# ScalarE's copies of the next weights among the squares, in the second down projection of a two-layer decoder trunk

## The chip, the cores and the metric

The kernel runs on one core of a Trainium2 chip. The metric is the device time of one execution in microseconds (us). TensorE's clock has two levels, 1.2 and 2.4 GHz; the profile gives the granted clock as a share of the higher one.

## What is computed

Two layers over 512 tokens of width 1024. Each layer has a token mixer (a gated linear recurrence in layer 0, attention with a forget bias in layer 1) and a squared-ReLU MLP with 4096 hidden features; each half is preceded by an RMS norm that is scaled and shifted by the conditioning vector. A last RMS norm ends it.

```
def sqrelu_mlp(h, w1, w2):
    a = jax.nn.relu(h @ w1)
    return (a * a) @ w2

for i in range(DEPTH):
    ...
    x = x + g1[:, None, :] * y
    h = modulate(x, norm2_w[i], sh2, sc2)
    x = x + g2[:, None, :] * sqrelu_mlp(h, mlp_w1[i], mlp_w2[i])
return rmsnorm(x, final_w)
```

The inputs are float32. The change concerns the last quarter of each MLP, the product with the second half of w2, and the sum of squares of the new x for the norm behind it.

## The kernel before

**Layout.** Activations lie transposed: features on the 128 partitions, the 512 tokens along the free dimension. x is 8 tiles of 128 features by 512 tokens. Every weight is cut into blocks of 128 x 1024 (512 KB), and four blocks are a quad; a layer has 26 quads, numbered through both layers. The blocks are streamed in one fixed order through four slots, j = 0 to 3, each with three buffers: `raw` (float32, from memory), `whi` (a copy in the matmul's reduced format, the high part) and `wlo` (raw less whi, the low part). Activations are split in the same way (h1hi and h1lo, a0hi and a0lo), and each product is three matmuls (lines 704 to 706): high by high, high weight by low activation, low weight by high activation. One block against one set of 8 activation tiles is 24 matmuls.

**The life of a slot.** SyncE loads raw[j] when the low part of the block before it in that slot has been made. ScalarE copies raw[j] to whi[j] when TensorE has ended the block that used the slot and the load has landed. GpSimd makes wlo[j] (line 622) behind that copy. TensorE waits for both before the block (`split`). The copy is the helper `hi_ahead`, lines 320 to 323:

```
def hi_ahead(quad, j):

    act.wait_ge(pe_blk, quad * 4 + j + 1)
    act.wait_ge(raw_in[j], quad * 16 + 32)
    S.activation(whi[:, j, :], raw[:, j, :], ACT.Copy).then_inc(w_hi, 1)
```

`pe_blk` counts TensorE's ended blocks. `hi_ahead(quad, j)` fills the slot that block j of this quad has just freed, for block j of the next quad. Each engine runs its own program in order; the order of ScalarE's operations is written out by hand.

**The MLP** (`mlp`, one function for each engine) has four stages, twice up and down: up projection of 16 hidden tiles (4 quads), down projection of these (4 quads), then the same for the other half of the hidden features. In a down projection a feature tile of the output needs two blocks, so a quad holds two features; feature t is summed in bank 4 + t % 2, and before it starts TensorE waits for VectorE's update of x with feature t - 2. In the first down projection of a layer ScalarE does nothing but `hi_ahead(q, j)` for each slot in turn, and VectorE updates x at line 1402.

**The second down projection** is part of `turnover(n, ...)`, with n = 2 in layer 0 and n = 4 in layer 1 (`from_w_out(n)` is false). It has four quads, q0 to q0 + 3. Features 0 to 5 are computed whole, from the first three quads; features 6 and 7, of the last quad, in two halves of 256 tokens. For each feature VectorE updates x (line 1335, `update`, counted in `x_upd`), ScalarE squares the new x (line 336, `square`, counted in `x_sq`; the first square goes to acc, the others to sqb) and VectorE adds the square to acc (line 1341, `added`, counted in `x_acc`). The sum goes to the norm that follows. The copies for the next quad stand among the squares in ScalarE's program: all four of them behind squares 1, 3 and 5, as the loop in the diff below shows. Copies for the quad q0 itself are made in the up projection's loop. VectorE's program for this stage and GpSimd's, which makes low parts in the order of the stream, don't depend on where ScalarE's copies stand. `turnover` with n = 1 and n = 3 follows the output projections of the mixers and takes the other branch.

Of the kernel before, what the change touches and what calls it, by code (L numbers as in the profile page):

```python
# [45 lines left out]
def build(nc, x_t, c_row, stream, mod_rows, w_forget, params, out_t):  # L46
    keep = ExitStack()
    with keep:
# [130 lines left out]
        def from_w_out(n):  # L179
            return n in (1, 3)  # L180
# [137 lines left out]
        def _(act):  # L318
# [6 lines that stand above are left out]
            def upper(n, th, first, end, h, shift):  # L325

                for k in range(first, end):
                    act.wait_ge(h_t, h_at(n, th, k))
                    S.activation(h[0][:, k, part(th)], t_buf(th, k), ACT.Identity,
                                 bias=mod[:, shift + k:shift + k + 1]).then_inc(h_hi, 1)  # L330

            def square(n, upd, i, add, t, cols_, dst):

                act.wait_ge(x_upd, upd)
                act.wait_ge(x_acc, add)
                S.activation(dst[:, cols_], x[:, t, cols_], ACT.Square).then_inc(x_sq, 1)

            def square_half(n, th, t):

                r, full_ = (0, 4) if from_w_out(n) else (2, 6)  # L340
                upd = UPD_AT[r + 3 * (n > 2)] + full_ + (KT - full_) * th + t - full_ + 1
                add = ADD_AT[n] + full_ - 1 + (KT - full_ - 1) * th + t - full_
                square(n, upd, 0, add, t, part(th), sqb)
# [75 lines left out]
            def turnover(n, q0, h, shift):  # L419

                all_ = slice(0, T)
                if from_w_out(n):
                    for j in range(4):
                        hi_ahead(q0, j)
                        square(n, UPD_AT[3 * (n > 2)] + j + 1, 0, ADD_AT[n] + max(j - 1, 0), j, all_, sqb if j else acc)
                    q0 += 1
                else:
                    for t in range(6):
                        square(n, UPD_AT[2 + 3 * (n > 2)] + t + 1, 0, ADD_AT[n] + max(t - 1, 0), t, all_, sqb if t else acc)
                        if t % 2:  # L430
                            for j in ((0, 1, 2, 3)):
                                hi_ahead(q0 + t // 2, j)
                    q0 += 3
                last_ = range(4, KT) if from_w_out(n) else range(6, KT)
                for t in last_:
                    square_half(n, 0, t)
                if from_w_out(n):
                    for j in range(2):
                        square_half(n, 1, 4 + j)
                        hi_ahead(q0, j)  # L440
                    upper(n, 0, 0, 3, h, shift)
                    square_half(n, 1, 6)
                    hi_ahead(q0, 2)
                    upper(n, 0, 3, 6, h, shift)
                    square_half(n, 1, 7)
                    hi_ahead(q0, 3)
                else:
                    if n == 4:
                        square_half(n, 1, 6)
                        square_half(n, 1, 7)  # L450
                        return
                    hi_ahead(q0, 0)
                    square_half(n, 1, 6)
                    hi_ahead(q0, 1)
                    upper(n, 0, 0, 3, h, shift)
                    hi_ahead(q0, 2)
                    upper(n, 0, 3, 6, h, shift)
                    square_half(n, 1, 7)
                    hi_ahead(q0, 3)
                upper(n, 0, 6, KT, h, shift)  # L460
                upper(n, 1, 0, KT, h, shift)

            def mlp(layer, a, h, shift):
                base = layer * LAYER_QUADS + Q_MLP
                for half in range(2):
                    with act.Fori(0, 4) as q:
                        for j in range(4):
                            act.wait_ge(pe_blk, (q + base + 8 * half) * 4 + j + 1)
                            ff_n = (q + 4 * half) * 4 + j + 32 * layer
                            if layer or half or j >= 2:  # L470
                                act.wait_ge(ff_lo, ff_n - 1)
                            S.activation(scr[j % 2][:, :], ps[j][:, :], ACT.Relu).then_inc(ff_r, 1)
                            hi_ahead(q + base + 8 * half, j)
                            act.wait_ge(ff_sq, ff_n + 1)
                            S.activation(tile(a[0], q * 4 + j), scr[j % 2][:, :], ACT.Copy).then_inc(ff_hi, 1)
                    if layer == 0 and half:
                        act.wait_ge(wf_in, 16)
                        S.activation(wfs[0][:, :], wf[:, :], ACT.Copy).then_inc(f_w, 1)
                    if half == 0:
                        with act.Fori(0, 4) as q:  # L480
                            for j in range(4):
                                hi_ahead(q + base + 4, j)
                turnover(2 * layer + 2, base + 12, h, shift)


            turnover(1, Q_OUT, h1, SH2)
            mlp(0, a0, h2, 48 + SH1)

# [62 lines left out]
            for s in range(GROUPS):  # L551
# [4 lines left out]
                for u in range(UNITS):  # L556
# [14 lines left out]
                    for s_, b in ended(s, u, FENDS):  # L571
                        fox_dense(s_, b)
            y_upper(GROUPS - 1)
            turnover(3, L + Q_OUT, h3, 48 + SH2)
            mlp(1, a1, None, None)

# [1049 lines left out]
```

## Time and profile before

| what | value |
|---|---|
| median of 3 runs | 1537.05 us (1536.89 to 1537.38) |
| the profiled execution, its own time | 1534.91 us |
| its span, first to last instruction | 1532.9 us |
| mean granted clock of TensorE | 0.973 |
| second down projection, layer 0 | about 655 to 765 us of the span |
| second down projection, layer 1 | about 1411 to 1522 us of the span |

Times in rows count from the start of the span. The profiled execution took 2.1 us less than the median of the runs. PE is TensorE, DVE is VectorE, ACT is ScalarE, POOL is GpSimd. In a timeline row the bracket tells how long the engine was idle before the operation and what ended the wait; "x4" stands for four operations of the same kind in a row, with the time from the first one's start to the last one's end.

### The profile page before, as it was taken

What the parts mean: (1) busy time and instruction counts of PE and PEld (TensorE: products, weight loads), DVE (VectorE), ACT (ScalarE), POOL (GpSimd) and SP (SyncE); (2) the same over time, 40 slices, a digit from 0 to 9 for tenths busy, and PEclk for the clock granted to TensorE, in tenths of its full rate; (3) what the DMA queues carried; (4) which work ended last, traced back from release to release, by engine and by line L of the source; (5) the groups of instructions that cost most, each with busy time, mean ns of one, the idle gap of its engine ahead of it and who ended that gap; (6) DMA issues with size and microseconds to landing.
All of it is one profiled execution on the core that took longest, in us unless ns stands there. A gap on an engine that the chain in (4) does not pass through costs nothing.

```text
span 1532.9 us, 21793 instructions
## 1 busy us (share of the span) xinstructions
PE 1432.9 (93%) x8088; PEld 1224.4 (80%) x8088; DVE 739.6 (48%) x1136; ACT 501.5 (33%) x770; POOL 690.6 (45%) x403
## 2 busy tenths in 40 slices
PE   2879999999999999988888999999999999999877
PEld 2678998989888888867887888887798888888667
DVE  7764647546796558821253333333457510254012
ACT  3513231414342123321244353535235321233120
POOL 8455748454465555532434333232144444443222
PEclk9889999999999999999999999999999999999998
DMA  9243333313265565521313121212032333223111
GB/s 376 92 145 127 116 137 111 134 45 102 105 219 192 183 212 192 207 82 55 85 69 110 56 87 53 97 42 63 9 109 85 101 93 93 94 96 96 55 55 56
DMA packets 47223, 169.95 MB, mean 111 GB/s; under 512 B 5024, under 2 KB 7200, under 8 KB 46384
## 3 DMA queue, kind: packets, MB, share of 16 engines
q1 hardware_dynamic: 46544, 164.73, 32.1%
q10 hardware_dynamic: 608, 4.23, 0.7%
q8 instruction: 50, 0.82, 0.2%
q14 instruction: 21, 0.17, 0.0%
HBM read 166.81 MB, written 2.13 MB: 110 GB/s over the span
## 4 chain that ended last, share of the span: by engine, by line
PE 41%; issue 33%; POOL 16%; DVE 7%; ACT 2%; DMA 1%; POOLq 0%; DVEq 0%; SPq 0%; ACTq 0%
POOL wlo L622 15%; PE bank L704 6%; PE bank L706 6%; PE bank L705 6%; PE bank L791 3%; PE bank L793 3%; PE bank L792 3%; PE bank L864 3%; PE bank L1032 3%; PE bank L1056 2%; PE bank L883 1%; PE bank L1043 1%; DVE modf L1239 1%; PE bank L1034 1%; DVE h2lo L1188 1%
## 5 line engine op out<-in xcount | busy, mean ns | idle before, releaser
L622 POOL TENSOR_TENSOR wlo<-raw,whi 128x1024 fp32r<-128x1024 f32 x208 | 540.7, 2607 | 691.2 <-ACT whi L323 691.1
L323 ACT ACTIVATE whi<-raw 128x1024 fp32r<-128x1024 f32 x204 | 213.1, 1054 | 180.0 <-PE bank L706 153.4
L1199 DVE CUSTOM_DVE_ANT_0 mring<-mring,cb 128x1024 f32<-128x1024 f32 x80 | 136.0, 1708 | 4.6 <-DMA mring<-mod_rows 4.6
L704 PE MATMUL bank<-a0hi,whi 128*128 128x512 f32 (+1 forms) x288 | 109.4, 380 | 15.2 <-POOL wlo L622 14.9
L704 PE MATMUL bank<-a1hi,whi 128*128 128x512 f32 (+1 forms) x288 | 109.5, 380 | 14.9 <-POOL wlo L622 14.9
L1335 DVE SCALAR_TENSOR_TENSOR x<-bank,mod,x 128x256 f32<-128x256 f32 (+1 forms) x44 | 26.5, 601 | 180.6 <-PE bank L706 180.6
L704 PE MATMUL bank<-h3hi,whi 128*128 128x512 f32 (+1 forms) x288 | 107.5, 373 | 2.2 <-DVE h3lo L1188 2.1
L704 PE MATMUL bank<-h1hi,whi 128*128 128x512 f32 (+1 forms) x288 | 107.1, 372 | 2.2 <-DVE h1lo L1188 2.1
L705 PE MATMUL bank<-a1lo,whi 128*128 128x512 f32 (+1 forms) x288 | 108.7, 377 | 0.0
L706 PE MATMUL bank<-a1hi,wlo 128*128 128x512 f32 (+1 forms) x288 | 108.7, 377 | 0.0
L706 PE MATMUL bank<-a0hi,wlo 128*128 128x512 f32 (+1 forms) x288 | 107.9, 375 | 0.0
L705 PE MATMUL bank<-a0lo,whi 128*128 128x512 f32 (+1 forms) x288 | 107.7, 374 | 0.0
L706 PE MATMUL bank<-h3hi,wlo 128*128 128x512 f32 (+1 forms) x288 | 107.0, 371 | 0.0
L705 PE MATMUL bank<-h3lo,whi 128*128 128x512 f32 (+1 forms) x288 | 106.9, 371 | 0.0
L705 PE MATMUL bank<-h1lo,whi 128*128 128x512 f32 (+1 forms) x288 | 106.0, 368 | 0.0
L706 PE MATMUL bank<-h1hi,wlo 128*128 128x512 f32 (+1 forms) x288 | 105.9, 368 | 0.0
L1480 DVE CUSTOM_DVE_ANT_0 scr<-bank,fb 128x128 f32<-128x128 f32 (+1 forms) x64 | 31.1, 487 | 154.1 <-issue 154.1
L791 PE MATMUL bank<-whi,h2hi 128*128 128x256 f32 x320 | 94.5, 295 | 3.3 <-POOL wlo L622 3.3
L704 PE MATMUL bank<-h0hi,whi 128*128 128x512 f32 x192 | 81.7, 425 | 15.8 <-DVE h0lo L1166 15.5
L793 PE MATMUL bank<-wlo,h2hi 128*128 128x256 f32 x320 | 91.2, 285 | 0.0
L792 PE MATMUL bank<-whi,h2lo 128*128 128x256 f32 x320 | 91.2, 285 | 0.0
L626 POOL TENSOR_TENSOR rst<-ssq,mhalf 128x2 f32<-128x2 f32 (+3 forms) x21 | 37.8, 1802 | 116.2 <-DVE ssq L1156 61.5
(241 smaller groups left out, 3359.7 us busy)
## 6 DMA issues: line engine op xcount, KB each, us to landing
raw<-stream SPq DMA_DIRECT2D x208, 512.0 KB, 3.8
mring<-mod_rows SPq DMA_DIRECT2D x80, 512.0 KB, 3.5
modf<-mod_rows SPq DMA_DIRECT2D x8, 1024.0 KB, 18.0
fb<-negf ACTq DMA_DIRECT2D x4, 1024.0 KB, 4.6
x<-x_t SPq DMA_DIRECT2D x2, 1024.0 KB, 8.0
out_t<-x SPq DMA_DIRECT2D x8, 256.0 KB, 2.2
cb<-c_row SPq DMA_DIRECT2D x1, 512.0 KB, 4.5
wf<-w_forget SPq DMA_DIRECT2D x1, 512.0 KB, 4.3
```

The source lines that it names most:

```text
L323: S.activation(whi[:, j, :], raw[:, j, :], ACT.Copy).then_inc(w_hi, 1)
L622: G.tensor_tensor(wlo[:, j, :], raw[:, j, :], whi[:, j, :].bitcast(F32), ALU.subtract).then_inc(w_lo, 1)
L626: G.tensor_tensor(rst[:, at:at + n], ssq[:, at:at + n], mhalf[:, 0:n], ALU.pow).then_inc(done, 1)
L704: PE.matmul(out, wh, hh[0], start=first, stop=False)
L705: PE.matmul(out, wh, hh[1], start=False, stop=False)
L706: return PE.matmul(out, wl, hh[0], start=False, stop=last)
L791: PE.matmul(o, hh, whi[:, j, w0], start=k == 0 and t % 2 == 0, stop=False, skip_group_check=True)
L792: PE.matmul(o, hl, whi[:, j, w0], start=False, stop=False, skip_group_check=True)
L793: mm = PE.matmul(o, hh, wlo[:, j, w0], start=False, stop=k == KT - 1, skip_group_check=True)
L864: mm = PE.matmul(second_halves(cols(ps[j], t), m), cols(kk, t), second_halves(cols(qq, t), m), start=True, stop=True)
L1032: PE.matmul(o[:, 0:n], qkT[0][r:r + DH, f, P * i:P * i + P], qkT[1][r:r + DH, f, 0:n], start=True, stop=False, skip_group_check=True)
L1199: V.tensor_tensor_reduce(out=mring[:, s, :], in0=mring[:, s, :], in1=cb[:, :], scale=1.0, scalar=0.0, op0=ALU.mult, op1=ALU.add, accum_out ...
```

## The change

In ScalarE's `turnover`, in the branch for n = 2 and n = 4, the twelve copies for quads q0 + 1 to q0 + 3 stand elsewhere: two of them ahead of each of the six squares, slots 0 and 1 ahead of an even feature's square, slots 2 and 3 ahead of an odd one's.

```
                 else:
                     for t in range(6):
+                        for j in (2 * (t % 2), 2 * (t % 2) + 1):
+                            hi_ahead(q0 + t // 2, j)
                         square(n, UPD_AT[2 + 3 * (n > 2)] + t + 1, 0, ADD_AT[n] + max(t - 1, 0), t, all_, sqb if t else acc)
-                        if t % 2:
-                            for j in ((0, 1, 2, 3)):
-                                hi_ahead(q0 + t // 2, j)
                     q0 += 3
```

The first place is ScalarE's program in layer 0, from the operation before the stage (the copy of wf) to the first square of a half feature. L323 are the copies to whi, L336 the squares. Before:

```order
L478 ACTIVATE wfhi<-wf 128x1024
L336 ACTIVATE acc<-x 128x512
L336 ACTIVATE sqb<-x 128x512
L323 ACTIVATE whi<-raw 128x1024 x4
L336 ACTIVATE sqb<-x 128x512 x2
L323 ACTIVATE whi<-raw 128x1024 x4
L336 ACTIVATE sqb<-x 128x512 x2
L323 ACTIVATE whi<-raw 128x1024 x4
L336 ACTIVATE sqb<-x 128x256 x2
```

And with the change:

```order
L477 ACTIVATE wfhi<-wf 128x1024
L323 ACTIVATE whi<-raw 128x1024 x2
L336 ACTIVATE acc<-x 128x512
L323 ACTIVATE whi<-raw 128x1024 x2
L336 ACTIVATE sqb<-x 128x512
L323 ACTIVATE whi<-raw 128x1024 x2
L336 ACTIVATE sqb<-x 128x512
L323 ACTIVATE whi<-raw 128x1024 x2
L336 ACTIVATE sqb<-x 128x512
L323 ACTIVATE whi<-raw 128x1024 x2
L336 ACTIVATE sqb<-x 128x512
L323 ACTIVATE whi<-raw 128x1024 x2
```

Behind these rows come the sixth square of 128x512 and the two of 128x256, as before. The twelve copies that stood in three groups of four now stand in six groups of two, each ahead of a square; a line lower in the program carries a number that is one less.

The second place is the same stage in layer 1, at the end of ScalarE's program, with the change:

```order
L465 COMPARE_AND_BRANCH
L323 ACTIVATE whi<-raw 128x1024 x2
L336 ACTIVATE acc<-x 128x512
...
L323 ACTIVATE whi<-raw 128x1024 x2
L336 ACTIVATE sqb<-x 128x512
L336 ACTIVATE sqb<-x 128x256 x4
```

There the copies follow on the loop of the up projection, and the last ones again stand ahead of the sixth square; the four squares of half features that end the program have not moved. The other engines' programs are the same.

## Rows read from the trace of the kernel before

**Rows 1.** page, part 1: busy time of each engine

```profile
PE 1432.9 (93%) x8088; PEld 1224.4 (80%) x8088; DVE 739.6 (48%) x1136; ACT 501.5 (33%) x770; POOL 690.6 (45%) x403
```

**Rows 2.** waits of TensorE, whole span: total us, times, longest

```profile
PE bank L704 <- POOL wlo L622: 29.8, 6, 5.0
```

**Rows 3.** timeline of VectorE, layer 0, second down projection: start, us, line, what [idle before]

```profile
674.14 0.75 DVE L1335 SCALAR_TENSOR_TENSOR x<-bank,mod,x 128x512 f32<-128x512 f32 x1 [10.23 <-PE bank L706]
675.58 0.69 DVE L1341 TENSOR_TENSOR acc<-acc,sqb 128x512 f32<-128x512 f32 x1 [0.69 <-ACT sqb L336]
692.80 0.75 DVE L1335 SCALAR_TENSOR_TENSOR x<-bank,mod,x 128x512 f32<-128x512 f32 x1 [16.53 <-PE bank L706]
...
703.79 0.75 DVE L1335 SCALAR_TENSOR_TENSOR x<-bank,mod,x 128x512 f32<-128x512 f32 x1 [8.85 <-PE bank L706]
...
721.36 0.75 DVE L1335 SCALAR_TENSOR_TENSOR x<-bank,mod,x 128x512 f32<-128x512 f32 x1 [15.43 <-PE bank L706]
...
732.35 0.75 DVE L1335 SCALAR_TENSOR_TENSOR x<-bank,mod,x 128x512 f32<-128x512 f32 x1 [8.85 <-PE bank L706]
...
745.52 0.48 DVE L1335 SCALAR_TENSOR_TENSOR x<-bank,mod,x 128x256 f32<-128x256 f32 x1 [11.03 <-PE bank L706]
...
751.17 0.48 DVE L1335 SCALAR_TENSOR_TENSOR x<-bank,mod,x 128x256 f32<-128x256 f32 x1 [4.26 <-PE bank L706]
```

**Rows 4.** timeline of ScalarE, the same stretch

```profile
674.92 0.63 ACT L336 ACTIVATE sqb<-x 128x512 f32<-128x512 f32 x1 [10.35 <-DVE x L1335]
675.46 3.88 ACT L323 ACTIVATE whi<-raw 128x1024 fp32r<-128x1024 f32 x4
```

**Rows 5.** timeline of GpSimd, the same stretch

```profile
676.58 9.35 POOL L622 TENSOR_TENSOR wlo<-raw,whi 128x1024 fp32r<-128x1024 f32 x4 [20.07 <-ACT whi L323]
```

**Rows 6.** timeline of TensorE, the first of the six waits

```profile
679.07 0.76 PE L704 MATMUL bank<-a0hi,whi 128*128 128x512 f32 x1 [4.97 <-POOL wlo L622]
```

**Rows 7.** windows of TensorE: us, busy (matmuls), granted clock, DMA share, GB/s

```profile
679.00:681.00 2.00, 1.93 (x5) 0.50 0.31 76
...
685.00:687.00 2.00, 2.00 (x10) 1.00 0.60 229
```

**Rows 8.** timeline of VectorE, layer 0, first down projection

```profile
487.22 0.75 DVE L1402 SCALAR_TENSOR_TENSOR x<-bank,mod,x 128x512 f32 x1 [6.28 <-PE bank L706]
...
564.10 0.75 DVE L1402 SCALAR_TENSOR_TENSOR x<-bank,mod,x 128x512 f32 x1 [5.75 <-PE bank L706]
```

**Rows 9.** timeline of ScalarE, layer 0, first down projection

```profile
486.97 1.06 ACT L323 ACTIVATE whi<-raw 128x1024 fp32r<-128x1024 f32 x1 [4.74 <-PE bank L706]
```

**Rows 10.** timeline of GpSimd, layer 0, first down projection

```profile
488.11 3.26 POOL L622 TENSOR_TENSOR wlo<-raw,whi 128x1024 fp32r<-128x1024 f32 x1 [3.40 <-ACT whi L323]
```

**Rows 11.** timeline of VectorE, layer 1, second down projection

```profile
1431.70 0.75 DVE L1335 SCALAR_TENSOR_TENSOR x<-bank,mod,x 128x512 f32<-128x512 f32 x1 [10.41 <-PE bank L706]
...
1450.58 0.75 DVE L1335 SCALAR_TENSOR_TENSOR x<-bank,mod,x 128x512 f32<-128x512 f32 x1 [16.74 <-PE bank L706]
...
1461.72 0.75 DVE L1335 SCALAR_TENSOR_TENSOR x<-bank,mod,x 128x512 f32<-128x512 f32 x1 [8.99 <-PE bank L706]
...
1479.36 0.75 DVE L1335 SCALAR_TENSOR_TENSOR x<-bank,mod,x 128x512 f32<-128x512 f32 x1 [15.50 <-PE bank L706]
...
1490.52 0.75 DVE L1335 SCALAR_TENSOR_TENSOR x<-bank,mod,x 128x512 f32<-128x512 f32 x1 [9.02 <-PE bank L706]
...
1503.52 0.48 DVE L1335 SCALAR_TENSOR_TENSOR x<-bank,mod,x 128x256 f32<-128x256 f32 x1 [10.87 <-PE bank L706]
...
1509.22 0.48 DVE L1335 SCALAR_TENSOR_TENSOR x<-bank,mod,x 128x256 f32<-128x256 f32 x1 [4.30 <-PE bank L706]
```

**Rows 12.** page, part 6: loads of weights, median us to landing

```profile
raw<-stream SPq DMA_DIRECT2D x208, 512.0 KB, 3.8
```

**Rows 13.** instructions by tile, a0lo: ns min/median/max, first and last start

```profile
L1429 DVE TENSOR_TENSOR a0lo<-scr,a0hi x32: 677/2884/2897, 406.3 to 656.4; 128x512 f32 x32
```

**Rows 14.** windows of TensorE after the turnover into layer 1

```profile
800.00:810.00 10.00, 9.78 (x68) 0.81 0.63 218
```

## The prediction

> **What bounds the kernel now.** Start with the busy shares: TensorE 93%, every other engine below half [rows 1]. A change that removes no TensorE work can therefore give back only time in which TensorE stands still or runs slowly, and the second view, the waits of TensorE, says where that is: 29.8 us in six waits, each close to 5.0 us, all on the low parts that GpSimd makes (line 622), all before line 704 [rows 2]. It is the largest entry that names one cause. GpSimd is only the last link, though, so the third view to read is the timeline of the other engines around one such wait. The second feature of the second down projection in layer 0 is complete when VectorE's update starts at 674.14 [rows 3]. The update lasts 0.75 us; ScalarE's square of that feature starts at 674.92, and behind it, at 675.46, four copies to whi in a row, 3.88 us [rows 4]. GpSimd starts its first subtraction at 676.58, four of them in 9.35 us [rows 5], and TensorE's next block starts at 679.07 after 4.97 us of idleness [rows 6]. Nothing in that chain of update, square, copy, subtraction is needed for the block by its data except the copy and the subtraction, and the slot that the copy fills had been free since the first of the quad's four blocks ended, three blocks earlier. ScalarE sat idle for 10.35 us before the square [rows 4] and GpSimd for 20.07 us before its subtraction [rows 5]: both had time, the order in ScalarE's program kept them from it.
>
> The stop costs more than it lasts. In the windows of TensorE the granted clock is 0.50 (its 1.2 GHz level) just after the stop, with 5 matmuls in 2 us, and 1.00 (2.4 GHz) six us later, with 10 [rows 7]. The clock fell after some 5 us without a matmul. So the loss of a stop is best read from the spacing of the updates, which holds both parts.
>
> The kernel also contains its own control. The first down projection has the same 24 matmuls a block, eight blocks of two quads after each other and the same engines, but ScalarE copies slot by slot there. Its eight updates run from 487.22 to 564.10 [rows 8], (564.10 - 487.22) / 7 = 10.98 us a feature, with three quad boundaries and no wait; each copy takes 1.06 us [rows 9] and each subtraction 3.26 us at the most [rows 10].
>
> **The change, part by part.** It adds and removes no instruction. In `turnover` for n = 2 and n = 4 it moves twelve copies each, from four behind squares 1, 3 and 5 to two ahead of each of squares 0 to 5. Every copy still waits for its slot and its load.
>
> The gain, layer 0 [rows 3]. Between two features of one quad the updates stand 703.79 - 692.80 = 10.99 us apart, like the control. Across the three boundaries: 692.80 - 674.14 = 18.66, so 7.67 lost; 721.36 - 703.79 = 17.57, so 6.58 lost; the third leads to a half feature, for which the spacing without a stop is 751.17 - 745.52 = 5.65, and it takes 745.52 - 732.35 = 13.17, so 7.52 lost. Sum 21.77 us. Layer 1 [rows 11], in the same way: a feature is 1461.72 - 1450.58 = 11.14, a half 1509.22 - 1503.52 = 5.70; lost are 18.88 - 11.14 = 7.74, 17.64 - 11.14 = 6.50 and 13.00 - 5.70 = 7.30. Sum 21.54 us. Together 43.3 us, of which 29.8 are the idle time [rows 2] and 13.5, or 2.2 a stop, the slow clock behind it.
>
> What has to be ready now. Slot j comes free when block j ends; copy 1.06 us [rows 9], subtraction at most 3.26 [rows 10], so its parts stand 4.3 us later, and TensorE wants them three blocks or 3 x 5.5 = 16.5 us later: 12 us of slack. Its next load can go out then and lands in 3.8 us [rows 12], at 8.1 us of a quad of 22.0: 13.9 us of slack. SyncE's queue keeps its order; its loads only go out earlier and one by one. GpSimd's four subtractions fill at most 13.0 of 22.0 us. I cost all of this at nothing; if the load's cover went, each quad would wait for what exceeds 13.9 us of lateness.
>
> What stands behind the moved copies: the squares. Copy 1 (or 3) and the update start at the end of the same block, so the square, which waited only for the update (0.75), now starts behind the copy (1.06): about 0.3 us later. Behind it VectorE has one addition to acc (0.69 us [rows 3]), then the update 10.98 us on; TensorE waits for that only to reuse a bank. The last pair is tighter: the half feature's update is due 5.65 us after the sixth feature, and copy, square and addition are 1.06 + 0.63 + 0.69 = 2.4 us. Nothing.
>
> One thing speaks against the move. VectorE's subtraction a0lo takes 0.68 us at the least and 2.88 in the median [rows 13], in the stage where GpSimd's subtractions run beside it. The moved copies put a GpSimd subtraction beside each of VectorE's additions, which had none before. I take the addition at up to 2.9 us in place of 0.69, 2.2 us more. The chain behind a feature is then 1.06 + 0.63 + 2.88 = 4.6 us, still under 5.65 and under 10.98, so the term stays nothing; with all six on TensorE's path in both layers it would be 12 x 2.2 = 26.4 us. The Trainium skill, "SBUF — State Buffer", section "SBUF: two separate sides", states that a VectorE operation with two SBUF inputs and a GpSimd operation that reads SBUF exclude each other on a shared port pair for a whole instruction, and by it the move would cost VectorE such waits at every addition that meets a subtraction. By that rule, the trace agrees that they exist (2.88 against 0.68 us); whether TensorE waits for them is for the chains above.
>
> Both ends of the unknown cost: below, 0, by the control; above, 26.4. I take 0, the control being the same work in the order that the change sets up.
>
> Sum: the profiled execution took 1534.9 us; 1534.9 - 43.3 = 1491.6. The median of the runs is 1537.05, 2.1 above that execution, so the forecast is 1537.05 - 43.3 = **1493.7 us**, -2.8%.
>
> **The rivals.**
> A. The waits go, the slow clock stays or comes back at another place: 1537.05 - 29.8 = 1507.2. For it: half clock shows in this kernel in other places too. Against: in the control's stage no such loss is seen between updates, and the slow windows that I read follow idle time [rows 7]. 3%.
> B. The shared port, as above, all on the path: 1493.7 + 26.4 = 1520.1. For it the 2.88 us; against it 4.6 us of chain under 10.98 us of time. 2%.
> C. Slower: the square, the addition and the update now stand behind copies that wait for loads, and TensorE waits for the updates before it reuses a bank: a ring. It costs something from the point where the chain behind a feature exceeds the 10.98 us until its bank is wanted. Were every load just late, so that a load, a subtraction, the copy and the rest stood in a row, it would be 3.8 + 3.26 + 1.06 + 1.06 + 0.63 + 2.88 + 0.75 = 13.4 us, with a landing half as long again (5.7) 15.3: 4.3 us of stop, 6.5 with the slow clock, at 12 features: 1493.7 + 78 = 1572. Against: a load has 13.9 us of slack. 1%.
> D. It does not do what it says, 1537: the copies would wait for something else as long. The program's order shows them ahead of the squares and their waits name only the slot and the load. 2%.
>
> **How the numbers follow.** The forecast gets 92%. Its own spread: the six stops, alike in idle time, lost 6.5 to 7.7 us, 1.2 us apart, which is how much the return of the clock differs from one stop to another; some slow stretches behind layer 0's turnover stay, as 0.81 of the clock in 800 to 810 [rows 14], and now begin at other moments. Three or four of them at 1.2 us give 4 to 5 us both ways, and 0.3 us for the runs themselves. The range is 1489.0 to 1500.0, a little longer upwards because a rest of a wait is likelier than a gain I have not counted. What A to D hold, 8%, lies outside, and some of the forecast's own. What a measurement of this kernel can tell from no change is about 0.2%, 3.1 us: faster 0.97 (forecast, A, B), same 0.02 (D), slower 0.01 (C).
>
> **What would show it.** In the new profile TensorE's six waits on line 622 before line 704 must be gone, two copies must lie ahead of each square, GpSimd's subtractions must stand 5.5 us apart in place of four in a row, and updates must come every 11.0 (layer 0) and 11.15 us (layer 1) across the boundaries, with a clock of 1.00 from the up projection to the norm. The additions to acc should be longer than 0.69 us where a subtraction runs: right if TensorE doesn't wait for them. The prediction is wrong if TensorE waits there for x updates, if copies wait for loads, if the spacing is closed but the clock stays at 0.5, or if what is gained in the two stages comes back as waits in the attention of layer 1.

## The result, and the profile after

The changed kernel takes 1495.72 us, the median of 4 runs (1492.69 to 1496.17); the kernel before beside it took 1536.97 us (1536.06 to 1537.38, 4 runs). The ratio is 0.9728 with a 95% interval of 0.9711 to 0.9745: 2.7% faster, 41.3 us between the medians. The forecast was 1493.7 us with a range of 1489.0 to 1500.0. The profiled execution took 1492.69 us, with a span of 1490.8 us and a mean granted clock of 0.984 (0.973 before).

The page of the changed kernel, the busy times and the chain that ended last:

```profile
PE 1420.5 (95%) x8088; PEld 1215.3 (82%) x8088; DVE 757.5 (51%) x1136; ACT 502.7 (34%) x770; POOL 690.7 (46%) x403
...
PE 86%; DVE 8%; ACT 2%; issue 2%; DMA 1%; POOL 0%; POOLq 0%; DVEq 0%; SPq 0%; ACTq 0%
```

TensorE's busy time has fallen by 12.4 us against [rows 1] though it does the same 8088 matmuls: most of that is the part of the loss that lay in slow matmuls. (It is good to some 4 us only: two more profiles of the changed kernel, below, have 1420.0 and 1423.9.) VectorE's has risen by 17.9 us; the additions to acc explain it, below. The chain of the kernel before, by engine:

```profile
PE 41%; issue 33%; POOL 16%; DVE 7%; ACT 2%; DMA 1%; POOLq 0%; DVEq 0%; SPq 0%; ACTq 0%
```

There GpSimd's subtractions (line 622) had 15% of the span.

The waits of TensorE, whole span (us in total, times, longest), the largest entries and those at the same line as [rows 2]:

```profile
PE bank L731 <- DVE acc L1254: 15.3, 1, 15.3
PE bank L703 <- DVE h0lo L1165: 14.1, 2, 8.6
...
PE bank L790 <- POOL wlo L621: 4.9, 2, 3.3
...
PE bank L703 <- DVE h3lo L1187: 2.7, 2, 1.7
...
PE bank L703 <- DVE h1lo L1187: 1.8, 1, 1.8
```

The entry of six waits and 29.8 us is gone: line 703 here is line 704 of the kernel before, and its waits are now on VectorE at other stages. ScalarE and GpSimd around the end of the second feature in layer 0, where [rows 4] and [rows 5] had four operations in a row (start, us, operation, idle time before it and its releaser):

```profile
669.94 1.06 ACT L323 ACTIVATE whi<-raw 128x1024 fp32r<-128x1024 f32 x1 [3.91 <-PE bank L705]
675.43 1.06 ACT L323 ACTIVATE whi<-raw 128x1024 fp32r<-128x1024 f32 x1 [4.43 <-PE bank L705]
676.39 0.61 ACT L336 ACTIVATE sqb<-x 128x512 f32<-128x512 f32 x1
680.92 1.06 ACT L323 ACTIVATE whi<-raw 128x1024 fp32r<-128x1024 f32 x1 [3.91 <-PE bank L705]
```

```profile
671.07 2.41 POOL L621 TENSOR_TENSOR wlo<-raw,whi 128x1024 fp32r<-128x1024 f32 x1 [3.09 <-ACT whi L323]
676.57 2.41 POOL L621 TENSOR_TENSOR wlo<-raw,whi 128x1024 fp32r<-128x1024 f32 x1 [3.09 <-ACT whi L323]
682.06 2.41 POOL L621 TENSOR_TENSOR wlo<-raw,whi 128x1024 fp32r<-128x1024 f32 x1 [3.09 <-ACT whi L323]
```

Each copy now waits for TensorE to end the block in its slot (the releaser is PE), not for an update of x, and the subtractions follow at 5.5 us. VectorE in layer 0, which answers to [rows 3], with the first update of the stage added:

```profile
664.44 0.75 DVE L1334 SCALAR_TENSOR_TENSOR x<-bank,mod,x 128x512 f32<-128x512 f32 x1 [4.24 <-PE bank L705]
675.43 0.75 DVE L1334 SCALAR_TENSOR_TENSOR x<-bank,mod,x 128x512 f32<-128x512 f32 x1 [10.24 <-PE bank L705]
677.04 2.48 DVE L1340 TENSOR_TENSOR acc<-acc,sqb 128x512 f32<-128x512 f32 x1 [0.86 <-ACT sqb L336]
686.42 0.75 DVE L1334 SCALAR_TENSOR_TENSOR x<-bank,mod,x 128x512 f32<-128x512 f32 x1 [6.90 <-PE bank L705]
...
719.38 0.75 DVE L1334 SCALAR_TENSOR_TENSOR x<-bank,mod,x 128x512 f32<-128x512 f32 x1 [6.90 <-PE bank L705]
720.99 2.47 DVE L1340 TENSOR_TENSOR acc<-acc,sqb 128x512 f32<-128x512 f32 x1 [0.86 <-ACT sqb L336]
724.82 0.48 DVE L1334 SCALAR_TENSOR_TENSOR x<-bank,mod,x 128x256 f32<-128x256 f32 x1 [1.35 <-PE bank L705]
...
730.26 0.48 DVE L1334 SCALAR_TENSOR_TENSOR x<-bank,mod,x 128x256 f32<-128x256 f32 x1 [4.05 <-PE bank L705]
```

The update behind the first quad boundary comes 686.42 - 675.43 = 10.99 us after the one before it, where it was 18.66, and from the first update to that of feature 7's first half the stage is 730.26 - 664.44 = 65.82 us long. In the kernel before, the stages began with these two updates, of layer 0 and of layer 1:

```profile
663.15 0.75 DVE L1335 SCALAR_TENSOR_TENSOR x<-bank,mod,x 128x512 f32<-128x512 f32 x1 [4.25 <-PE bank L706]
...
1420.54 0.75 DVE L1335 SCALAR_TENSOR_TENSOR x<-bank,mod,x 128x512 f32<-128x512 f32 x1 [6.58 <-PE bank L706]
```

Layer 0's stage took 751.17 - 663.15 = 88.02 us there. Layer 1 with the change, answering to [rows 11]:

```profile
1400.11 0.75 DVE L1334 SCALAR_TENSOR_TENSOR x<-bank,mod,x 128x512 f32<-128x512 f32 x1 [6.58 <-PE bank L705]
1411.26 0.75 DVE L1334 SCALAR_TENSOR_TENSOR x<-bank,mod,x 128x512 f32<-128x512 f32 x1 [10.40 <-PE bank L705]
...
1422.42 0.75 DVE L1334 SCALAR_TENSOR_TENSOR x<-bank,mod,x 128x512 f32<-128x512 f32 x1 [7.07 <-PE bank L705]
...
1467.40 0.48 DVE L1334 SCALAR_TENSOR_TENSOR x<-bank,mod,x 128x256 f32<-128x256 f32 x1 [4.37 <-PE bank L705]
```

It takes 1467.40 - 1400.11 = 67.29 us, where it was 1509.22 - 1420.54 = 88.68. So the two stages gave back 22.20 + 21.39 = 43.6 us in this profile. The span shrank by 42.1: the first stage began 1.3 us later and the stretch between the two stages took 0.5 us more, the tail 0.3 less, though the work there is the same.

### The profile page after: what moved, and what is told of

Same layout as the page of the kernel before. It is cut to its first block, busy times and chain, and to the rows that moved or that the text cites. A ratio compares the mean times of both kernels' runs of the same rounds, so it can differ in the third digit from the quotient of the medians.

```text
span 1490.8 us, 21793 instructions
## 1 busy us (share of the span) xinstructions
PE 1420.5 (95%) x8088; PEld 1215.3 (82%) x8088; DVE 757.5 (51%) x1136; ACT 502.7 (34%) x770; POOL 690.7 (46%) x403
## 4 chain that ended last, share of the span: by engine, by line
PE 86%; DVE 8%; ACT 2%; issue 2%; DMA 1%; POOL 0%; POOLq 0%; DVEq 0%; SPq 0%; ACTq 0%
PE bank L703 21%; PE bank L705 20%; PE bank L704 20%; PE bank L790 3%; PE bank L792 3%; PE bank L791 3%; PE bank L863 3%; PE bank L1031 3%; PE bank L1055 2%; PE bank L882 1%; PE bank L1042 1%; DVE modf L1238 1%; DVE h3lo L1187 1%; DVE scr L1182 1%; PE bank L1033 1%
## 5 line engine op out<-in xcount | busy, mean ns | idle before, releaser
L323 ACT ACTIVATE whi<-raw 128x1024 fp32r<-128x1024 f32 x204 | 215.4, 1056 | 278.5 <-PE bank L705 252.9
L703 PE MATMUL bank<-a1hi,whi 128*128 128x512 f32 (+1 forms) x288 | 106.5, 370 | 0.0
L703 PE MATMUL bank<-a0hi,whi 128*128 128x512 f32 (+1 forms) x288 | 105.8, 367 | 0.3
L471 ACT ACTIVATE scr<-bank 128x512 f32<-128x512 f32 x64 | 38.0, 594 | 156.5 <-PE bank L705 156.5
## 6 DMA issues: line engine op xcount, KB each, us to landing
modf<-mod_rows SPq DMA_DIRECT2D x8, 1024.0 KB, 17.9
```

Of the source, the lines that this page charges most:

```text
L703: PE.matmul(out, wh, hh[0], start=first, stop=False)
```

## The experiments

All were run beside the kernel before; its median is given with each group. The first four share one chip, with 1536.22 us for the kernel before (7 runs).

**Slot 0 alone.** What has to be early: all four copies, or the first?

```
                     for t in range(6):
                         square(n, ...)
-                        if t % 2:
-                            for j in ((0, 1, 2, 3)):
-                                hi_ahead(q0 + t // 2, j)
+                        for j in ((0,), (1, 2, 3))[t % 2]:
+                            hi_ahead(q0 + t // 2, j)
```

> Only the copy of slot 0 is moved: it stands behind the square of the quad's first feature, the copies of slots 1 to 3 stay behind the square of the second. Theory (TensorE stops because the next quad's first block has no low part; the other three are in time even from the old place): slot 0 is ready before the boundary, slot 1 needs square 1.4, copy 1.06, subtraction 2.4 = 4.9 us behind the boundary and is wanted at 5.5, so no stop: 1495.7 us, the change's time, within 2 us. Rival (the four copies and subtractions in a burst are what costs, so the burst must be spread): three of four parts of the loss stay, about 1527 us.

Measured: 1499.19 us (1497.93 to 1501.04), ratio 0.9756 (0.974 to 0.9773). The rival's 1527 is out, but the time is 4.8 us above the change's 1494.40 in the same group, so the theory missed something. TensorE's waits, and VectorE's updates across the last boundary of layer 0:

```profile
PE bank L703 <- POOL wlo L621: 4.3, 2, 2.2
```

```profile
721.21 0.75 DVE L1334 SCALAR_TENSOR_TENSOR x<-bank,mod,x 128x512 f32<-128x512 f32 x1 [8.84 <-PE bank L705]
...
729.26 0.48 DVE L1334 SCALAR_TENSOR_TENSOR x<-bank,mod,x 128x256 f32<-128x256 f32 x1 [5.91 <-PE bank L705]
...
734.91 0.48 DVE L1334 SCALAR_TENSOR_TENSOR x<-bank,mod,x 128x256 f32<-128x256 f32 x1 [3.89 <-PE bank L705]
```

Two waits of 2.2 us are left, one a layer. At the other four boundaries none is, and updates come at 10.99 us in layer 0. At the last one the next quad is done in halves: a half block lasts 2.8 us, so slot 1 is wanted 2.8 us behind the boundary and not 5.5, and its low part comes at 4.9. The spacing is 729.26 - 721.21 = 8.05 in place of 5.65; with 8.07 in place of 5.70 in layer 1 that is the whole 4.8 us. So one early copy buys all of it where a block is 5.5 us long, and the theory holds with the deadline of each slot taken from the next quad, not from the present one.

**Behind the feature's own square.** Two copies a feature, as in the change, but behind the square.

```
                     for t in range(6):
-                        for j in (2 * (t % 2), 2 * (t % 2) + 1):
-                            hi_ahead(q0 + t // 2, j)
                         square(n, ...)
+                        for j in (2 * (t % 2), 2 * (t % 2) + 1):
+                            hi_ahead(q0 + t // 2, j)
```

> The two copies of a feature's slots stand behind that feature's square, not ahead of it: 1.4 us later each, with 12 us of slack. Theory: the change's time, 1495.7 us within 2 us, with the squares 0.5 us earlier than in the change and the additions to acc at another point of GpSimd's subtraction. Rival (it matters that the copies are ahead of the square): a rest of the wait stays at the six boundaries, up to 1.4 us each and more with the clock, 1504 us or above.

Measured: 1493.69 us (1491.42 to 1495.07), ratio 0.9722 (0.9705 to 0.9739), the same as the change. ScalarE and VectorE behind the second feature of layer 0:

```profile
675.61 0.63 ACT L336 ACTIVATE sqb<-x 128x512 f32<-128x512 f32 x1 [8.46 <-DVE x L1334]
676.15 1.99 ACT L323 ACTIVATE whi<-raw 128x1024 fp32r<-128x1024 f32 x2
```

```profile
676.27 0.69 DVE L1340 TENSOR_TENSOR acc<-acc,sqb 128x512 f32<-128x512 f32 x1 [0.70 <-ACT sqb L336]
```

The addition to acc takes 0.69 us here, since it is over before GpSimd starts (677.27); in the change it takes 2.48. That makes no difference to the time. On which side of a square the copies stand does not matter. What matters, by this run and the one before, is that the copies of the slots wanted first, slot 0 and at the last boundary slot 1 too, stand ahead of the second feature's square, whose update comes only at the end of the quad.

**The stop filled.** The kernel before, with 20 matmuls whose result nobody reads in each of TensorE's three stops of a layer.

```
                             feature_block(q + base + 8 * half + 4, j, 4 + j // 2, a, k0=KT * (j % 2),
                                           first=j % 2 == 0, last=j % 2 == 1)
+                        if half:
+                            for _ in range(20):
+                                PE.matmul(ps[7][:, :], a[0][:, 0, 0:P], a[0][:, 1, :], start=True, stop=True)
```

> The kernel before, with 20 matmuls behind each of the first three quads of the second down projection whose result nobody reads (some 4.6 us at full clock, where TensorE would stand still for 4.97). The stop stays as long as it was, only TensorE isn't idle in it. Theory (about 2.2 us of each of the six losses is the clock that has fallen to 0.5 in the stop): the clock stays at 1.00 and the time falls by 13.5 us although work is added, to 1523.5 us. Rival (the 2.2 us are something else behind the boundary, such as the loads and subtractions that run then): the time stays at 1537 us or rises.

Measured: 1525.27 us (1524.75 to 1526.96), ratio 0.9932 (0.9915 to 0.9948): faster by 10.9 us with 120 matmuls more, all of 512 columns. TensorE's waits, its windows around the first restart (us, busy and matmuls, granted clock, DMA share, GB/s), and VectorE's updates:

```profile
PE bank L704 <- POOL wlo L622: 2.9, 6, 0.5
```

```profile
678.00:680.00 2.00, 1.50 (x7) 1.00 0.00 0
680.00:682.00 2.00, 2.00 (x10) 1.00 0.88 240
```

```profile
674.23 0.75 DVE L1338 SCALAR_TENSOR_TENSOR x<-bank,mod,x 128x512 f32<-128x512 f32 x1 [10.24 <-PE bank L706]
...
690.50 0.75 DVE L1338 SCALAR_TENSOR_TENSOR x<-bank,mod,x 128x512 f32<-128x512 f32 x1 [14.13 <-PE bank L706]
...
701.49 0.75 DVE L1338 SCALAR_TENSOR_TENSOR x<-bank,mod,x 128x512 f32<-128x512 f32 x1 [8.85 <-PE bank L706]
```

The low part is as late as before (TensorE restarts at 679.23, 5.0 us after the update at 674.23), the clock is 1.00 where [rows 7] had 0.50, and the boundary costs 690.50 - 674.23 - 10.99 = 5.28 us in place of 7.67. From first update to last the stages take 82.08 and 82.95 us, 11.7 less than before in all. So of the 13.5 us that I put down to the clock, 11.7 are the clock, and 1.8 (0.3 a stop) stay at full clock. About half of this 0.3 is how the stop was measured: at full clock a matmul here lasts 0.39 us and the next one starts 0.23 us behind it, so an idle time counted from the end of one to the start of the next leaves out 0.16 us of overlap. The rest is not resolved. That the loads or subtractions behind the boundary cost the time is refuted: they run there as before.

**The changed kernel again.**

> The changed kernel again, for its spread and a second profile. Theory: 1495.7 us, within the 1492.7 to 1496.2 us seen; single executions differ by 3 us because the slow clock at the start and behind layer 0's turnover lasts longer or shorter, so this profile's stages of the second down projection should take 65.8 and 67.3 us from the first update to the last as before, and what differs should lie outside them.

Measured: 1494.40 us (1493.53 to 1495.16), ratio 0.9729 (0.9713 to 0.9746). The stages took 65.82 and 67.40 us, as expected. A second repetition, on another chip:

> The changed kernel beside it on the same chip: 1494.5 to 1495.5 us, 41 to 43 us under the kernel before.

Measured: 1493.61 us (1492.36 to 1495.89) beside 1536.81 (9 runs), ratio 0.9713 (0.9695 to 0.9732). Its span is 1493.5 us, 2.7 us longer than the first profile's 1490.8. The stages took 66.24 and 67.39 us, 0.5 more; 1.7 us more lie between them. TensorE at the turnover into the last MLP, in this profile and in the first one of the changed kernel:

```profile
1120.00:1130.00 10.00, 9.77 (x61) 0.69 0.30 100
```

```profile
1120.00:1130.00 10.00, 8.61 (x71) 1.00 0.26 97
```

Much the same short waits stand ahead of both (1.8 and 0.8 us in the repetition, where the clock is 0.69; 1.7, 0.7 and 1.0 in the first profile, where it is 1.00). Whether a short idle time costs the clock differs here from one execution to the next.

The next four share a chip, with 1537.55 us for the kernel before (7 runs).

**One layer alone.**

```
+                        if n == 2:
+                            for j in (2 * (t % 2), 2 * (t % 2) + 1):
+                                hi_ahead(q0 + t // 2, j)
                         square(n, ...)
-                        if t % 2:
+                        if n == 4 and t % 2:
                             for j in ((0, 1, 2, 3)):
                                 hi_ahead(q0 + t // 2, j)
```

(The second pair of lines is the old order, which layer 1 keeps.)

> The change in layer 0 alone (n = 2); layer 1 keeps the old order. Theory (six alike losses of some 7.2 us, three a layer, independent of each other): 21.8 us less than before, 1515.2 us, three waits of 5.0 us left on the low parts, in layer 1. Rival (the gain of one layer comes back as a wait in the attention of layer 1, and what the change gained was made in the other): well above or below half, by more than 4 us.

Measured: 1515.44 us (1515.04 to 1516.17), ratio 0.986 (0.9844 to 0.9877), 22.1 us less, half of the whole. Of the waits three are left:

```profile
PE bank L707 <- POOL wlo L625: 14.9, 3, 5.0
```

The two layers' stops are alike and independent, and nothing that layer 0 gains is paid back in layer 1.

**More additions on VectorE.** The changed kernel with two more additions a feature on VectorE, ahead of each addition to acc.

```
                     if t:
+                        if not from_w_out(n):
+                            dve.wait_ge(x_sq, SQ_AT[n] + t + 1)
+                            for i in range(2):
+                                V.tensor_tensor(scr[i][:, :], sqb[:, :], sqb[:, :], ALU.add)
                         added(SQ_AT[n] + t + 1, all_)
```

> The changed kernel, with two more additions of the same shape on VectorE ahead of each addition to acc in this stage, whose results nobody reads. The addition now takes 2.48 us where it took 0.69, held up by GpSimd's subtraction. Theory (VectorE has 11 us a feature there, and TensorE waits for its updates only when a bank is reused): two more cost nothing, 1495.7 us within 2 us, though only 0.1 us or so is left at the half feature's update. Rival (the port shared by VectorE and GpSimd is already on TensorE's path): 1.4 us or more for each of the 10 features, 1510 us or above.

Measured: 1494.12 us (1493.12 to 1494.85), ratio 0.972 (0.9704 to 0.9737), as the change. VectorE at the tightest place, behind the sixth feature:

```profile
721.98 3.08 DVE L1354 TENSOR_TENSOR scr<-sqb 128x512 f32<-128x512 f32 x2 [0.86 <-ACT sqb L336]
724.98 0.68 DVE L1340 TENSOR_TENSOR acc<-acc,sqb 128x512 f32<-128x512 f32 x1
726.02 0.48 DVE L1334 SCALAR_TENSOR_TENSOR x<-bank,mod,x 128x256 f32<-128x256 f32 x1 [0.36 <-PE bank L705]
```

With two more additions VectorE is done 0.36 us before the half feature's update is due; in the change it waits 1.35 us for that. An addition that meets a subtraction costs VectorE time, and the kernel none.

**The same idea at another place.** At the start of layer 1's attention the change leaves a wait of 3.3 us on a low part (line 790 above). The copy stands in ScalarE's program behind three activations of the forget gate. Three steps, each on top of the one before; first the copy (`fox_dense(-1, 2)` holds nothing else) ahead of the gate:

```
+            fox_dense(-1, 2)
             act.wait_ge(f_pe, 1)
             S.activation(gs[:, 0, :], ps[0][:, :], ACT.Abs, ...)
             ...
-            fox_dense(-1, 2)
             fox_dense(-1, 3)
```

> The changed kernel, and the same idea at one more place: at the start of layer 1's attention the copy of quad 27's slot 0 stands behind three activations for the forget gate and two table loads, and TensorE then waits 3.27 us for its low part. Here the copy stands ahead of them. Theory: that wait goes, but the next wait, for VectorE's normed q (1.15 us before the first transposes), grows by what is gained less the copy's 0.95 us, since its chain begins behind the same activations: 1 to 2 us gained, 1494 us. Rival (TensorE's wait was the bound): 3.3 us and the slow clock behind it, 5 us or more, 1490 us.

Measured: 1491.75 us (1490.43 to 1493.0), ratio 0.9706 (0.969 to 0.9722).

```profile
PE bank L1018 <- DVE qt L1468: 4.1, 1, 4.1
```

The wait on the low part of 3.3 us is gone and the one for the norm of q has grown from 1.1 to 4.1 us, as the theory had it. The one for the norm of k (3.2) is gone, and two on ScalarE are new, 2.3 us for qT and 0.9 for qt. Together the waits are 7.3 us, where the change had 7.6. The median lies 1.9 to 4.0 us under the three medians of the change, between the theory's 1494 and the rival's 1490, but the profile does not show this as a gain of the step. The stretch that holds the attention runs from the update of feature 7's first half in layer 0 to the first update of layer 1's stage:

```profile
727.69 0.48 DVE L1336 SCALAR_TENSOR_TENSOR x<-bank,mod,x 128x256 f32<-128x256 f32 x1 [4.26 <-PE bank L707]
...
1398.67 0.75 DVE L1336 SCALAR_TENSOR_TENSOR x<-bank,mod,x 128x512 f32<-128x512 f32 x1 [6.58 <-PE bank L707]
```

It took 1398.67 - 727.69 = 670.98 us, and 669.85, 670.92 and 671.58 in the three profiles of the change. This execution was ahead before it came to the edit: its first stage began at 661.45, theirs at 663.66 to 664.62. So the wait moved and no gain of this step is shown. Second, q ahead of the gate on both engines, and the gate's round trip behind k:

```
 # ScalarE; forget_gate() is its three activations for the gate
             fox_dense(-1, 2)
-            forget_gate()
             fox_dense(-1, 3)
-            act.wait_ge(f_out, 1)
-            act.dma_start(fscr, gs[0:HEADS, 1, :]).then_inc(f_dram, 16)
+            forget_gate()
             fox_dense(-1, 4)
-            act.wait_ge(f_dram, 16)
-            forget(0)
             fox_dense(-1, 5)
+            act.wait_ge(f_out, 1)
+            act.dma_start(fscr, gs[0:HEADS, 1, :]).then_inc(f_dram, 16)
             fox_dense(-1, 6)
+            act.wait_ge(f_dram, 16)
+            forget(0)
 # VectorE; forget_sums() is its part of the gate up to the running sum
-            forget_sums()
             sums(0, 0)
             normed(0, 0)
+            forget_sums()
             sums(0, 1)
             normed(0, 1)
```

> As the one before, and ScalarE's evacuation of q and VectorE's norm of q stand ahead of the forget gate's chain, and the broadcast of the gate's sums is sent after the evacuation of k. Theory: q's chain starts 5 us earlier, so both the wait for the low part (3.27 us) and the one for q (1.15) go, and the wait for k (3.23 us) stays or moves by a little, since its norm is held by GpSimd's subtractions and its root: 4 to 6 us gained over the change with the clock, 1490.5 us. Rival (the gate's sums, which the first scores need through a round trip in memory, come too late): new waits on them and no gain, 1495 us or above.

Measured: 1491.07 us (1489.28 to 1492.96), ratio 0.9707 (0.9691 to 0.9723), by the medians not told apart from the step before.

```profile
PE bank L1018 <- DVE kt L1469: 6.5, 1, 6.5
```

The waits for the low part, q and k had become one of 6.5 us for the norm of k. The stretch took 1396.45 - 728.95 = 667.50 us, 2.4 to 4.1 less than in the change: this step gained, if less than the 4 to 6 us of the theory. Third, on VectorE the sums of squares of k ahead of the gate:

```
             normed(0, 0)
-            forget_sums()
             sums(0, 1)
+            forget_sums()
             normed(0, 1)
```

> The kernel with the gate behind q, and on VectorE the sums of squares of k ahead of the forget gate's sums, so that GpSimd's root of them runs beside the gate's sums. In the kernel with the gate behind q all waits of TensorE at this place had merged into one of 6.5 us for the norm of k. Theory (that norm is what TensorE waits for, and it is held by the order on VectorE): the wait falls to about 3.5 us, 3 us less than there, 1488 us, and 6 to 7 us less than the change. Rival (the first scores then wait for the gate's sums from memory): the same as there, 1491 us.

Measured, beside the second repetition of the change: 1487.84 us (1487.55 to 1489.34), ratio to the kernel before 0.9678 (0.9661 to 0.9696), and 5.8 us under the change's 1493.61 on the same chip.

```profile
787.53 0.63 PE L1018 MATMUL bank<-ident,qt 128*128 128x128 f32 x4 [1.18 <-ACT qT L531]
790.20 0.66 PE L1018 MATMUL bank<-ident,kt 128*128 128x128 f32 x4 [2.03 <-DVE kt L1469]
```

The wait for k fell from 6.5 to 2.0 us, with one of 1.2 for q's evacuation ahead of it, 3.2 in all; the theory had said about 3.5. The stretch of the attention took 1394.87 - 730.47 = 664.40 us, 3.1 less than in the step before and 5.5 to 7.2 less than in the change. That is room enough for the 5.8 us between the medians, and the theory's 1488 is met. This kernel has the lowest median of all.

## Why the prediction was right

- **What bounds the kernel** was right: the six waits had one cause, and both engines that stood in the chain had time. The two stages gave back 43.6 us in the first profile against 43.3 in the sum; layer 0 22.2 against 21.8, layer 1 21.4 against 21.5.
- **Idle time and clock.** The split into [rows 2] and the rest, 29.8 + 13.5, was nearly right: the filled stop puts 11.7 us on the clock and leaves 1.8, about half of it the overlap that an idle time leaves out. The sum didn't depend on the split, because it was made from the spacing of updates.
- **The control** was the strongest argument. Its 10.98 us is the new spacing in layer 0 (10.99), and every 10 us window of TensorE from 660 to 770 us now has a clock of 1.00; in layer 1 the spacing is 11.16 us and the clock 1.00 up to 1480 us.
- **The edits costed at nothing** were nothing. The subtractions took 2.41 us where I allowed 3.26; the additions 2.48 where I allowed 2.88, and ten of them 1.79 us longer each are the 17.9 us by which VectorE's busy time rose. The chain behind the sixth feature ended 723.46 - 719.38 = 4.1 us after its end (I had 4.6), before the 5.4 at which the next update came. In the rows after the change the addition of 677.04 begins inside the subtraction of 676.57 to 678.98 and ends at 679.52, 0.54 us behind it: it ran behind it and not beside it. By the rule on the shared port that the prediction takes from the Trainium skill, "SBUF — State Buffer", section "SBUF: two separate sides", the trace agrees. Rival B as a time is refuted by the run with more additions. One slip stood in its price: I counted 12 additions, but the first square of a stage goes to acc without one, so there are ten, and the bound was 22.0 us and not 26.4.
- **Rivals A, C and D** did not happen: no slow clock in the stages, no waits for updates in them, and each copy released by its slot.
- **The size.** Between medians the gain was 41.3 us in the first comparison and 41.8 and 43.2 in the two repetitions; 2.0, 1.5 and 0.1 us less than 43.3. Each interval of the ratio has room for 43.3, so no missing term is shown. What there is of it in the profiles lies outside the stages: the first profile lost 1.5 us there, net, and two profiles of the changed kernel differ by 2.7 us with 1.7 of it between the stages. The stretch between the stages took 669.37 us in the profile that the sum started from and 669.85 to 671.58 in the three of the change, but also 671.63 in the kernel with the filled stops, which has the old order. So these differences are not shown to come from the change. The range had allowed for them (stretches of slow clock that stay and begin at other moments), and the time stayed within.

One step of the working was wrong without harm, and the run with slot 0 alone brought it out: I had given every slot three full blocks, 16.5 us, and 12 us of slack, but behind the last boundary a block is done in halves, and three of them are some 8.2 us. In the change slot 3 is the tight one there. Its block ends with the sixth feature, at 719.38, and this is its subtraction:

```profile
720.52 2.40 POOL L621 TENSOR_TENSOR wlo<-raw,whi 128x1024 fp32r<-128x1024 f32 x1 [3.09 <-ACT whi L323]
```

It ends at 722.92, and TensorE wants it three half blocks behind 719.38, at about 727.5. The slack is between 4 and 5 us, and the forecast did not suffer.

## What to carry to other kernels

When the tensor engine waits for a prepared operand, look at what stands ahead of the preparing operation in its own engine's program, not only at the engine named: an in-order engine that was idle and then did four ready operations in a burst is the sign. Price such a stop from the spacing of the work across it, against a stage that does the same work without it, and check each slot's deadline against the work that comes next. Removing a wait pays in full where the stage behind it has slack, as here, and moves to the next chain where it has none, as at the start of the attention: there the first step removed a wait of 3.3 us and lowered the sum of the waits by 0.3. The median of that run, 1.9 us or more lower, hides it: compare the stretch that holds the edit, not only the whole.

## What the runs showed of the hardware

Matmuls without a use made the kernel before faster by 10.9 us, because TensorE kept its 2.4 GHz through stops of 5 us in which it otherwise fell to 1.2 GHz. At full clock a stop cost 0.3 us more than its idle time shows, about half of it because matmuls of 0.39 us start 0.23 us apart. An addition on VectorE took 2.48 us where it met a subtraction on GpSimd and 0.69 us where it did not. And the chain that ended last is no measure of a price: GpSimd's subtractions had 15% of it before and GpSimd has 0% now, for 2.7% of the time.
